# An S5 and attention network in fp32: scan result left in its PSUM bank, GpSimd's product one unit later, and reordered jobs in five stages

## Chip, core and metric

The kernel runs on one core of a Trainium2 chip. The metric is the device time of one execution in microseconds (us); of several runs the median is taken. Engines: PE is TensorE, DVE is VectorE, ACT is ScalarE, POOL is GpSimd, SP issues most DMAs.

## What is computed

Two networks one after the other, on 256 tokens (T) of 1024 features (D), all in fp32. Only the S5 mixer is shown in full; the rest is named.

```python
x = first_block(x, c, ...)    # ada-modulated: conv + retention mixer, FFN (f1.0, f2.0), S5 mixer + GLU, FFN (f1.1, f2.1)
return second_block(x, mem_2, ...)  # gated linear attention, forgetting attention, attention into mem, gates, FFN
...
def _mixer_s5(h, lam_re, lam_im, log_step, b_re, b_im, c_re, c_im, d_skip, w_glu_a, w_glu_b):
    # x_t = a * x_(t-1) + B u_t (complex diagonal a), in both directions of time; y_t = Re(C x_t) + d u_t
    ...
    return (z @ w_glu_a) * jax.nn.sigmoid(z @ w_glu_b)      # z = gelu(y)
```

## The kernel before

The program has one hand-written instruction stream per engine, with semaphores between them. On PE every job (a group of matmuls into one PSUM bank) has its place in a list (`job_order`), and bank number = turn modulo the number of banks; `begin` waits until the bank's former reader is done, and `job_wait` on another engine waits for a job's end. Weights come by DMA on SP's queue into a ring of three slots of 2 MB ("panels"). A matmul of exact fp32 value is made of three fast ones: ACT copies the high part (`split_high`, L874), DVE subtracts it for the low part (`split_low`, L1346), and `project_split` runs high x high, high x low, low x high. Every such unit thus needs ACT, then DVE, then PE.

Stages in order of time, with the span's us of the profiled execution: modulation vectors (`ada`, DVE `ada_acc` L1290/L1293), the conv and retention mixer (to about 173), its output projection `wo0` (173 to 210), the norm `ms1` (219), FFN `f1.0` and `f2.0` (230 to 470), `ms2`, the S5 mixer (482 to 573), GLU (573 to 622), `ms3`, `mk`, the second FFN (653 to 850), the projections and the attentions (850 to 1014), gates, output and last FFN.

**S5 tables.** POOL computes for each of 8 slabs k the powers of a, the x part and the c part (L711, L714, L719); PE turns them into weights (`wt{k}`, transposes) and lags (`kl{k}`, the products that make the within-block convolution), in `s5_weights(k)`, of which the jobs stand between those of `wo0`, `f1.0` and `f2.0` (`S5_AFTER`, `SIDE_S5`). They need POOL's part of that slab (`tab_step`).

**S5 loop.** `uu` puts the input h into blocks. Then come 16 units n, two for each slab k:

- PE `drive(n)`: 32 matmuls of 64x64 into bank `v{n}`.
- DVE (loop at L1531): two products of the bank with a rotation table (L1542, L1543) into `pbuf`.
- POOL (loop at L768): the add of the two (L774) into `wbuf`.
- DVE: the scan (L1553) from `wbuf` with the decay rows that ACT writes (L998) into `gbuf`; and one product of it with the table (L1557).
- POOL: the other product (L781) of `gbuf`.
- PE `outputs(n)`: 64 matmuls of 64x63 over both products, accumulated in bank 6 or 7 with the within-block part. For odd n ACT then takes GELU (L1020), and `natural(k)` (jobs `z{k}`) puts tokens in order again, for the GLU.

PE's order in the loop is `outputs(n)`, `drive(n+3)`, and for even n from 2 on `natural(n/2-1)`. POOL's and DVE's order in it is

```python
for n in range(17):      # POOL, L768
    if n < 16: ...       # wait s5p 2n+2; wbuf = pbuf[0] + pbuf[1]     (add of unit n)
    if n >= 1: ...       # m = n-1; wait s5g m+1; product of unit m
for n in range(17):      # DVE, L1531
    if n < 16: ...       # two products of unit n
    if n >= 1: ...       # m = n-1; scan and product of unit m
    if n >= 5 and n % 2: z_low((n - 5) // 2)
```

`KEEP_BUSY` names jobs before which PE multiplies into a bank nobody reads while it waits.

Of the kernel before, what the change touches and what calls it, by code (L numbers as in the profile page):

```python
# [20 lines left out]
P = 128  # L21
T = 256
# [21 lines left out]
KEEP_BUSY = {"f1.0.0": 4, "uu0": 6, "ga0": 4, "ms3": 6}  # L44
# [16 lines left out]
ADA_AFTER = {3: 10, 6: 11, 8: 12, 11: 13, 13: 14, 15: 15}  # L61
# [3 lines left out]
S5_AFTER = {4: 2, 10: 3, 15: 4}  # L65
SIDE_ADA = {0: 16, 1: 17, 3: 18, 4: 19, 5: 20, 6: 21}
SIDE_S5 = {1: 5, 3: 6, 5: 7}


def job_order():  # L70
# [4 lines left out]
            "wo0.0", "ada7", "wo0.1", "wt0.0", "kl0", "wt0.1", "ada8", "wo0.2", "ada9", "wo0.3", "wt1.0", "kl1", "wt1.1", "ms1"]  # L75
    for j in range(16):
        jobs.append(f"f1.0.{j}")
        if j in ADA_AFTER:
            jobs.append(f"ada{ADA_AFTER[j]}")
        if j in S5_AFTER:  # L80
            k = S5_AFTER[j]
            jobs += [f"wt{k}.0", f"kl{k}", f"wt{k}.1"]
    for b in range(8):
        if b in SIDE_ADA:
            jobs.append(f"ada{SIDE_ADA[b]}")
        if b in SIDE_S5:
            k = SIDE_S5[b]
            jobs += [f"wt{k}.0", f"kl{k}", f"wt{k}.1"]
    jobs += [f"f2.0.{p}" for p in range(4)] + ["ms2"]
    jobs += [f"uu{q}" for q in range(4)] + [f"v{n}" for n in range(3)] + [f"dd{q}" for q in range(4)]  # L90
    for n in range(16):
        if n + 3 < 16:
            jobs.append(f"v{n + 3}")
        if n >= 2 and n % 2 == 0:
            jobs.append(f"z{n // 2 - 1}")
        if n == 11:
            jobs.append("mms")
# [3 lines left out]
    for j in range(2, 16):  # L101
        jobs.append(f"f1.1.{j}")
        if j in (5, 9):
# [3 lines left out]
             "nr0", "nr1", "fk1", "cs0", "cs1", "at0", "at1", "go0", "gor0", "nr2", "nr3", "go1", "gor1",  # L107
             "fv0", "fv1", "mq0", "mq1"]
    bg = 0
    for u in range(10):  # L110
# [4 lines left out]
        if u in (0, 1):  # L115
            jobs.append(f"nr{4 + u}")
# [6 lines left out]
    for p in range(1, 6):  # L123
# [9 lines left out]
ROOTS = ["ms0", "rr0", "rr1", "var", "ms1", "ms2", "mms", "ms3", "mkr0", "mkr1", "ms4", "ms5", "nr0", "nr1", "gor0",  # L133
         "nr2", "nr3", "gor1", "nr4", "nr5", "ms6"]
BANKS = 6
LATE_WEIGHTS = tuple(f"{name}" for k in (5, 6, 7) for name in (f"wt{k}.0", f"kl{k}", f"wt{k}.1"))
ROTATING = [name for name in JOBS if not name.startswith("ada") and name not in LATE_WEIGHTS]
# [3 lines left out]
def build(nc, a, out):  # L141

    ctx = ExitStack()
    with ctx:
# [192 lines left out]
        ffn_panels(0)  # L337
        for i in range(2):
            cols_panel(f"ga{i}", a["w_glu_a"], 512 * i, 512, f"ga{2 * i + 1}")
            cols_panel(f"gb{i}", a["w_glu_b"], 512 * i, 512, f"gb{2 * i + 1}")  # L340
            if i == 0:
                panels.append(("mem", a["mem"].rearrange("(k p) t -> p k t", p=P), KT, T, ("memn", None)))
# [71 lines left out]
        high_bufs = [split["ada_slot0"][:, 0:2048], split["ada_slot0"][:, 2048:4096], split["prep"][:, 0:2048]]  # L414
# [63 lines left out]
        freed = {f"ms{n}": ("rstd", n + 1) for n in range(7)}  # L478
        for j in range(2):
# [5 lines left out]
                          f"go{j}": ("gon", 2 * j + 2), f"gor{j}": ("gors", j + 1), f"fv{j}": ("fvc", j + 1)})  # L485
# [21 lines left out]
        def c_steps(k):  # L507
# [5 lines left out]
                      "kot": ("koc", 1), "cs0": ("gst", 5), "cs1": ("gst", 3)})  # L513
        freed.update({f"nr{i}": ("nrs", i + 1) for i in range(6)})
# [38 lines left out]

        def ada_in(k):
# [25 lines left out]
        def _(sp):  # L580
# [3 lines left out]
            for k in range(EARLY_ADA):  # L584
                sp.dma_start(ada_slot(k), ada_source(k)).then_inc(ada_in(k)[0], 16)  # L585
# [27 lines left out]
            for i, (name, src, k, n, _) in enumerate(panels):  # L613
# [26 lines left out]
                if name == "mem":  # L640
# [12 lines left out]
        def _(pool):  # L653
# [72 lines left out]
            for k in range(8):  # L726
# [18 lines left out]
                if k:  # L745
                    pool.wait_ge(s("wout_out"), 16 * k)
                pool.wait_ge(s("tab_step"), done)
# [20 lines left out]
            for n in range(17):  # L768
# [22 lines left out]
        def _(act):  # L791
# [44 lines left out]
            def split_high(u):  # L836
# [28 lines left out]
                elif u in (GATES, GATES + 1):  # L865
# [21 lines left out]
            ada_load(act, 6)  # L887
            for j in range(2):
                job_wait(act, f"ag{j}")
# [1604 lines left out]
```

## Time and profile before

| | |
|---|---|
| median of 3 runs | 1332.55 us (1329.34 to 1334.72) |
| profiled execution | 1337.0 us, span 1335.2 us |
| mean granted PE clock | 0.956 of full |
| busy PE / DVE / ACT / POOL | 1233.7 / 856.9 / 530.6 / 410.0 us |
| HBM | 192 GB/s over the span |

All rows below are of that one profiled execution, in us from the start of its span. A row gives the start, the busy time, engine, line, operation with output<-inputs by tile, and in brackets the idle time before it and what ended that. PEclk is the granted share of TensorE's full clock. Matmuls overlap, so the step from one to the next is its cost, not its own duration.

### The profile page before, as it was taken

Reading aid. Unit: us, or ns where it says so; the run is one execution under the profiler, and the core shown is the slowest. Engines: PE = TensorE matmul, PEld = TensorE weight load, DVE = VectorE, ACT = ScalarE, POOL = GpSimd, SP = SyncE. Lnnn points to the kernel's source line nnn. Section 1 sums busy time; section 2 is a strip of 40 time slices with the busy share of each in tenths; the row PEclk is TensorE's granted clock in tenths of the full one; section 3 lists DMA queues with packets and bytes.
Section 4 is the critical chain, followed back from the end, with each engine's and each line's share of the span. In section 5 each row is a group of like instructions: output and inputs, shape, how many; then the busy total and the mean of one; then the engine's idle time right before and its main releaser. Section 6 shows DMA issues by size and latency. Waiting matters only on the chain.

```text
span 1335.2 us, 24456 instructions
## 1 busy us (share of the span) xinstructions
PE 1233.7 (92%) x10696; PEld 1143.0 (86%) x10696; DVE 856.9 (64%) x946; ACT 530.6 (40%) x663; POOL 410.0 (31%) x573
## 2 busy tenths in 40 slices
PE   4898897999998878898999999998998999999998
PEld 4785685999998848787899999698787999999998
DVE  6699963886567558845597543556856467556553
ACT  2130232444233244343455432448267644544241
POOL 7999638398788218700000000000000012000000
PEclk7899898999998889999999999999798999999999
DMA  9962667588977645256265554345141445455551
GB/s 349 389 256 94 236 219 262 187 306 304 338 286 273 225 138 172 75 171 229 68 249 190 189 179 175 122 156 190 43 147 64 151 166 189 161 174 177 182 192 64
DMA packets 120251, 258.20 MB, mean 193 GB/s; under 512 B 5056, under 2 KB 19024, under 8 KB 120016
## 3 DMA queue, kind: packets, MB, share of 16 engines
q1 hardware_dynamic: 91184, 196.18, 41.8%
q10 hardware_dynamic: 25504, 46.81, 9.6%
q0 software_dynamic: 3456, 13.63, 2.7%
q8 instruction: 85, 1.39, 0.4%
q14 instruction: 22, 0.18, 0.0%
HBM read 241.93 MB, written 14.68 MB: 192 GB/s over the span
## 4 chain that ended last, share of the span: by engine, by line
PE 68%; DVE 11%; POOL 8%; DMA 5%; issue 3%; ACT 3%; SPq 1%; DVEq 0%; POOLq 0%; ACTq 0%
PE bank L1864 68%; DVE big L1403 4%; POOL tabw L714 2%; POOL tabw L711 2%; POOL big L781 2%; DMA ring<-in_w_in 1%; DMA ada_slot<-in_ada_w 1%; DVE ada_acc L1293 1%; POOL prep L719 1%; DMA ring<-in_w_fc 1%; DVE rstd L1303 1%; POOL big L774 1%; SPq L585 1%; DVE ring_split L1346 1%; ACT ada_slot_split L874 1%
## 5 line engine op out<-in xcount | busy, mean ns | idle before, releaser
L1864 PE MATMUL bank<-squares_split,ring_split 128*128 128x256 f32 x1056 | 300.7, 285 | 0.0
L1864 PEld LDWEIGHTS bank<-squares_split,ring_split 128*128 128x128 f32 x1056 | 204.5, 194 | 0.0
L787 POOL TENSOR_TENSOR y_cat<-y_cat,tmp 128x512 f32<-128x512 f32 x8 | 11.1, 1388 | 536.9 <-DVE tmp L1782 536.9
L1293 DVE SCALAR_TENSOR_TENSOR ada_acc<-ada_slot,cact,ada_acc 128x512 f32<-128x512 f32 x152 | 126.9, 835 | 5.1
L1864 PE MATMUL bank<-ada_slot_split,ring_split 128*128 128x256 f32 x432 | 122.2, 283 | 0.0
L1346 DVE TENSOR_TENSOR ring_split<-ring,ada_slot_split 128x2048 fp32r<-128x2048 f32 (+1 forms) x32 | 72.1, 2257 | 56.9 <-ACT ada_slot_split L874 56.9
L1864 PE MATMUL bank<-big_split,ring_split 128*128 128x256 f32 x352 | 100.1, 284 | 0.0
L1303 DVE RECIPROCAL rstd<-bank 128x512 f32<-128x512 f32 (+1 forms) x21 | 56.0, 2668 | 51.1 <-ACT bank L805 51.0
L1864 PE MATMUL bank<-big_split,ada_slot_split 128*128 128x256 f32 x296 | 85.5, 289 | 0.0
L1864 PEld LDWEIGHTS bank<-ada_slot_split,ring_split 128*128 128x128 f32 x432 | 82.9, 192 | 0.0
L1346 DVE TENSOR_TENSOR ring_split<-ring,tabw_split 128x2048 fp32r<-128x2048 f32 x22 | 50.4, 2291 | 49.6 <-ACT tabw_split L874 49.6
L1864 PE MATMUL bank<-h_in_split,ada_slot_split 128*128 128x256 f32 x272 | 78.2, 287 | 3.6 <-DVE ring_split L1346 2.2
L874 ACT ACTIVATE ada_slot_split<-ring 128x2048 fp32r<-128x2048 f32 (+1 forms) x32 | 60.3, 1885 | 49.1 <-PE bank L1864 27.8
L1864 PE MATMUL bank<-h_in,ring 128*128 128x256 f32 x320 | 74.0, 394 | 2.6 <-ACT h_in L829 2.6
L1346 DVE TENSOR_TENSOR ring_split<-ring,y_cat_split 128x2048 fp32r<-128x2048 f32 x21 | 50.3, 2396 | 38.5 <-ACT y_cat_split L874 38.5
L1864 PE MATMUL bank<-big_split,tabw_split 128*128 128x256 f32 (+1 forms) x264 | 74.7, 283 | 0.0
L1864 PEld LDWEIGHTS bank<-h_in,ring 128*128 128x128 f32 x320 | 63.3, 199 | 12.0 <-issue 2.7
L1346 DVE TENSOR_TENSOR ring_split<-ring,tmp_split 128x2048 fp32r<-128x2048 f32 x20 | 47.5, 2375 | 33.0 <-ACT tmp_split L874 33.0
L1864 PE MATMUL bank<-squares_split,tmp_split 128*128 128x256 f32 x208 | 62.6, 301 | 6.1 <-DVE h_in_split L1338 5.6
L1864 PEld LDWEIGHTS bank<-big_split,ring_split 128*128 128x128 f32 x352 | 68.0, 193 | 0.0
L874 ACT ACTIVATE tabw_split<-ring 128x2048 fp32r<-128x2048 f32 x22 | 42.0, 1909 | 45.8 <-PE bank L1864 29.1
L1864 PE MATMUL bank<-squares_split,y_cat_split 128*128 128x256 f32 x208 | 59.5, 286 | 0.0
(420 smaller groups left out, 3879.9 us busy)
## 6 DMA issues: line engine op xcount, KB each, us to landing
ring<-in_w_fc SPq DMA_DIRECT2D x32, 2048.0 KB, 8.7
ada_slot<-in_ada_w ACTq DMA_DIRECT2D x20, 2048.0 KB, 10.5
ring<-in_w_in SPq DMA_DIRECT2D x19, 2048.0 KB, 8.2
ring<-in_w_ffn_gate SPq DMA_DIRECT2D x5, 2048.0 KB, 7.8
ring<-in_w_ffn_up SPq DMA_DIRECT2D x5, 2048.0 KB, 7.9
ring<-in_w_ffn_down SPq DMA_DIRECT2D x5, 2048.0 KB, 7.8
ring<-in_w_out SPq DMA_DIRECT2D x4, 2048.0 KB, 7.7
ring<-in_w_branch SPq DMA_DIRECT2D x3, 2048.0 KB, 7.8
```

What stands on the lines that cost most here:

```text
L585: sp.dma_start(ada_slot(k), ada_source(k)).then_inc(ada_in(k)[0], 16)
L711: step(pool.tensor_tensor(part.rearrange("p (d m c) -> p d m c", d=2, m=8), before, real[:, n_].rearrange("p (d q) r -> p d (q r)", d=2).u ...
L714: step(pool.tensor_tensor(both[:, 128 * d:128 * d + 128].rearrange("p (q r c) -> p q r c", q=4, r=2), one_way(view, steps, e - 1, d)[:, :, ...
L719: step(pool.tensor_tensor(by_step(view, n, steps, e), x_parts[:, 0:256].rearrange("p (d m c) -> p d m c", d=2, m=8), x_parts[:, 256:512].r ...
L774: pool.tensor_tensor(wbuf[n % 2], pb[:, 0], pb[:, 1], ALU.add).then_inc(s("s5w"), 1)
L781: pool.tensor_tensor(rotated(m)[:, 1], gbuf[m % 2][:, :, ::-1, :], tab[:, :, 2:0:-1, :], ALU.mult).then_inc(s("s5r"), 1)
L874: act.activation(high, whole, ACT.Copy).then_inc(s("w_high"), 1)
L1293: stt(acc, w[:, i, :], cact[:, i:i + 1], acc, ALU.mult, ALU.add)\
L1303: return dve.reciprocal(rs[:, 0:width], ps(job)[:, 0:width]).then_inc(s(sem), 1)
L1346: tt(low, whole, high.bitcast(F32), ALU.subtract).then_inc(s("w_low"), 1)
L1403: stt(conv[:, i, :], src, w, conv[:, i, :], ALU.mult, ALU.add).then_inc(s("conv"), 1)
L1864: return pe.matmul(*args, skip_group_check=True, **kw)
```

## The change

It has one part in the S5 loop and several in other stages.

1. S5 loop. DVE's scan writes its result into bank `v{m}` (free by then) instead of `gbuf`, and its product reads it there. ACT copies the bank to `gbuf` (`scanned`), POOL's product reads that copy, and POOL's loop takes it with m=n-2 instead of n-1. The `z` jobs use the other half of banks 6 and 7; the low parts `z_low` come two units later. PE's order in the loop is the same.
2. Before the loop. `mms` (mean square of the memory input) moves from inside the loop to ahead of `uu`; `uu` is done in two halves of the features; the memory panel is loaded earlier.
3. Start. The DMAs of the first four ada panels come in two halves; DVE's `s5_scalars` moves ahead of `ada_acc(4)`.
4. Around `wo0`. `wt` and `kl` are separate jobs, both of slab 0 ahead of `wo0.0`; `wo0.0` and `wo0.1` are interleaved (`project_pair`), as are `f1.0.0` and `f1.0.1`; `ms1` is ahead of slab 1; in `f1.0` and `f2.0` `kl{k}` stands some units behind `wt{k}`. POOL issues the DMA of the `bc` table after the x part.
5. `ms3`. ACT squares before it splits the next weights. `KEEP_BUSY` is smaller, and gone for `ga0`.
6. Projections. `fv` goes ahead of `gla_out(0)`; six roots of norms are kept in SBUF instead of a bank; DVE's order of splits and head norms is changed.

The diff, cut to its core:

```diff
-KEEP_BUSY = {"f1.0.0": 4, "uu0": 6, "ga0": 4, "ms3": 6}
+KEEP_BUSY = {"f1.0.0": 2, "uu0": 4, "ms3": 2}
...
+WT_AFTER = {2: 2, 6: 3, 10: 4, 14: 5}
+KL_AFTER = {4: 2, 8: 3, 12: 4}
...
-            "wo0.0", "ada7", "wo0.1", "wt0.0", "kl0", "wt0.1", "ada8", "wo0.2", "ada9", "wo0.3", "wt1.0", "kl1", "wt1.1", "ms1"]
+            "wt0.0", "wt0.1", "kl0", "wo0.0", "wo0.1", "ada7", "ada8", "wo0.2", "ada9", "wo0.3", "ms1", "wt1.0", "wt1.1", "kl1"]
...
         # POOL
-            for n in range(17):
+            for n in range(18):
                 if n < 16:
                     pool.wait_ge(s("s5p"), 2 * n + 2)
...
-                if n >= 1:
-                    m = n - 1
+                if n >= 2:
+                    m = n - 2
                     tab = tabs[m // 2 % 3][:, 4 * (m % 2):4 * (m % 2) + 4]
-                    pool.wait_ge(s("s5g"), m + 1)
+                    pool.wait_ge(s("s5c"), m + 1)
...
         # ACT
+            def scanned(n):
+
+                act.wait_ge(s("s5q"), n + 1)
+                if n >= 2:
+                    act.wait_ge(s("s5r"), n - 1)
+                act.activation(gbuf[n % 2].rearrange("p q c t -> p (q c t)"), ps(f"v{n}")[:, :], ACT.Copy).then_inc(s("s5c"), 1)
...
+            squares(3, False)
             split_high(SECOND)
+            root("ms3")
...
         # DVE
                     dve.wait_ge(s("s5w"), m + 1)
-                    if m >= 2:
-                        dve.wait_ge(s("s5r"), m - 1)
                     dve.wait_ge(s("decay"), 4 * m + 4)
-                    flat = (view.rearrange("p q c t -> p (q c t)") for view in (gbuf[m % 2], wbuf[m % 2]))
-                    result, source = flat
+                    source = wbuf[m % 2].rearrange("p q c t -> p (q c t)")
+                    result = ps(f"v{m}")[:, :]
                     dve.tensor_tensor_scan(result, decays[m % 3], source, 0.0, ALU.mult, ALU.add).then_inc(s("s5g"), 1)
...
-                    tt(rotated(m)[:, 0], gbuf[m % 2], tab[:, :, 0:1, :].broadcast_to([P, 4, 2, 64]), ALU.mult).then_inc(s("s5q"), 1)
-                if n >= 5 and n % 2:
-                    z_low((n - 5) // 2)
+                    scan = result.rearrange("p (q c t) -> p q c t", q=4, c=2)
+                    tt(rotated(m)[:, 0], scan, tab[:, :, 0:1, :].broadcast_to([P, 4, 2, 64]), ALU.mult).then_inc(s("s5q"), 1)
+                if n >= 6 and n % 2 == 0:
+                    z_low((n - 6) // 2)
...
         # PE
-            for i in range(2):
-                w = panel(f"wo{i}")
-                for j in range(2):
-                    project(f"wo0.{2 * i + j}", w, 2 * j, yt3, cat_ready, order=(4, 5, 6, 7, 0, 1, 2, 3))
+            s5_weights(0)
+            s5_lags(0)
+            w = panel("wo0")
+            project_pair(("wo0.0", "wo0.1"), w, yt3, cat_ready, (4, 5, 6, 7, 0, 1, 2, 3))
+            ada(7)
+            ada(8)
+            w = panel("wo1")
+            project("wo0.2", w, 0, yt3, no_wait)
+            ada(9)
+            project("wo0.3", w, 2, yt3, no_wait)
+            mean_squares(1)
+            s5_weights(1)
+            s5_lags(1)
```

**Order on POOL in the S5 loop, before** (units 2 to 5; `big` holds `pbuf`, `wbuf`, `gbuf` and the products; the second row is the first unit's product):

```order
L774 TENSOR_TENSOR big<-big 128x512 [waits s_s5p] x2
L781 TENSOR_TENSOR big<-big,tabw 128x512 [waits s_s5g]
L774 TENSOR_TENSOR big<-big 128x512 [waits s_s5g,s_s5p]
L781 TENSOR_TENSOR big<-big,tabw 128x8x64 [waits s_s5g]
L774 TENSOR_TENSOR big<-big 128x512 [waits s_s5g,s_s5p]
```

and now:

```order
L794 TENSOR_TENSOR big<-big 128x512 [waits s_s5p] x2
L794 TENSOR_TENSOR big<-big 128x512 [waits s_s5g,s_s5p]
L801 TENSOR_TENSOR big<-big,tabw 128x512 [waits s_s5c]
L794 TENSOR_TENSOR big<-big 128x512 [waits s_s5g,s_s5p]
L801 TENSOR_TENSOR big<-big,tabw 128x8x64 [waits s_s5c]
```

The first unit's product (the first row with `tabw`) had two adds ahead of it and now has three; so it goes for every unit.

**Order on PE in the S5 loop, now** (64x63 are outputs, 64x64 over `squares,ada_slot` a drive, over `squares,prep` the within-block part of an even unit, 32x64 `natural`; the 48 ahead are the drives of units 0 to 2; line L1864 of before is L1932):

```order
L1932 MATMUL bank<-squares,ada_slot 64x64 x48
L1932 MATMUL bank<-prep,s_select 128x512 x16
L1932 MATMUL bank<-squares,prep 64x64 x8
L1932 MATMUL bank<-big,ada_slot 64x63 x32
L1932 MATMUL bank<-squares,ada_slot 64x64 x16
L1932 MATMUL bank<-big,ada_slot 64x63 x32
L1932 MATMUL bank<-squares,ada_slot 64x64 x16
```

Before has the same rows in the same order: after unit 0's outputs the drive of unit 3, after unit 1's that of unit 4.

**Order on PE around `wo0`, before** (`y_cat,ring` is `wo0`, `ident,tabw` is `wt`, `prep` with 32x64 is `kl`, `one,ada_acc` is `ada`, `squares,inv` is `ms1`):

```order
L1864 MATMUL bank<-y_cat,ring 128x256 x16
L1864 MATMUL bank<-one,ada_acc 128x1 x4
L1864 MATMUL bank<-y_cat,ring 128x256 x16
L1864 MATMUL bank<-ident,tabw 64x64 x16
L1864 MATMUL bank<-prep 32x64 x16
L1864 MATMUL bank<-ident,tabw 64x64 x16
L1864 MATMUL bank<-one,ada_acc 128x1 x4
L1864 MATMUL bank<-y_cat,ring 128x256 x16
```

and now:

```order
L1932 MATMUL bank<-ident,tabw 64x64 x32
L1932 MATMUL bank<-prep 32x64 x16
L1932 MATMUL bank<-y_cat,ring 128x256 x32
L1932 MATMUL bank<-one,ada_acc 128x1 x8
L1932 MATMUL bank<-y_cat,ring 128x256 x16
L1932 MATMUL bank<-one,ada_acc 128x1 x4
L1932 MATMUL bank<-y_cat,ring 128x256 x16
L1932 MATMUL bank<-squares,inv 128x256 x8
```

Slab 0's `wt` and `kl` moved from behind `wo0.1` to ahead of `wo0.0`, and `ada8` from behind them to right behind the pair.

## Rows read from the trace of the kernel before

**Rows 1.** The page: busy time by engine, chain that ended last.

```profile
PE 1233.7 (92%) x10696; PEld 1143.0 (86%) x10696; DVE 856.9 (64%) x946; ACT 530.6 (40%) x663; POOL 410.0 (31%) x573
...
PE 68%; DVE 11%; POOL 8%; DMA 5%; issue 3%; ACT 3%; SPq 1%; DVEq 0%; POOLq 0%; ACTq 0%
```

**Rows 2.** Busy time by stage: stretch, length, busy by engine, PEclk, DMA.

```profile
200.00:243.00 43.00, 32.51 (x230) 27.13 (x229) 22.29 (x28) 12.29 (x21) 37.92 (x60) 0.84 0.58 206
400.00:470.00 70.00, 61.99 (x631) 61.10 (x630) 45.49 (x47) 19.13 (x19) 38.94 (x42) 0.90 0.69 253
500.00:574.00 74.00, 62.94 (x1836) 58.63 (x1833) 61.76 (x64) 31.67 (x79) 53.55 (x29) 0.95 0.37 115
...
626.00:654.00 28.00, 21.36 (x90) 18.13 (x89) 14.95 (x21) 14.81 (x21) 0.00 (x0) 0.88 0.23 86
930.00:1014.00 84.00, 73.59 (x392) 58.20 (x393) 62.18 (x59) 38.34 (x50) 0.00 (x0) 0.86 0.26 92
...
512.00:552.00 40.00, 33.97 (x1111) 32.09 (x1109) 37.90 (x42) 19.76 (x58) 33.80 (x18) 1.00 0.51 161
```

**Rows 3.** Timeline of PE, S5 loop: start, duration, instruction.

```profile
518.10 2.09 PE L1864 MATMUL bank<-big,ada_slot 64*64 64x63 f32 x64 [1.34 <-POOL big L781]
519.99 1.14 PE L1864 MATMUL bank<-squares,ada_slot 64*64 64x64 f32 x32
...
522.39 2.21 PE L1864 MATMUL bank<-big,ada_slot 64*64 64x63 f32 x63 [0.68 <-POOL big L781]
...
526.48 0.74 PE L1864 MATMUL bank<-big,ada_slot 64*64 64x63 f32 x18 [0.42 <-POOL big L781]
```

**Rows 4.** Timeline of DVE, the same pass.

```profile
521.17 0.69 DVE L1542 TENSOR_TENSOR big<-bank,tabw 128x512 f32<-128x512 f32 x1
...
522.37 1.22 DVE L1553 TENSOR_TENSOR_SCAN big<-ada_acc,big 128x512 f32<-128x512 f32 x1
523.62 1.58 DVE L1557 TENSOR_TENSOR big<-big,tabw 128x512 f32<-128x512 f32 x1
```

**Rows 5.** Timeline of POOL, the same pass; and L774 over the loop.

```profile
522.53 2.12 POOL L774 TENSOR_TENSOR big<-big 128x512 f32<-128x512 f32 x1 [0.29 <-DVE big L1543]
524.61 1.72 POOL L781 TENSOR_TENSOR big<-big,tabw 128x512 f32<-128x512 f32 x1
...
L774 POOL TENSOR_TENSOR big<-big x16: 1259/2115/2122, 493.1 to 559.9; 128x512 f32<-128x512 f32 x16
```

**Rows 6.** Timeline of PE: outputs(0), outputs(13), first GLU job.

```profile
499.88 0.33 PE L1864 MATMUL bank<-big,ada_slot 64*64 64x63 f32 x5
...
559.02 2.08 PE L1864 MATMUL bank<-big,ada_slot 64*64 64x63 f32 x64
...
573.52 0.57 PE L1864 MATMUL bank<-h_in_split,ada_slot_split 128*128 128x256 f32 x1
```

**Rows 7.** Timeline of PE: an outputs and a drive after a wait.

```profile
508.20 3.15 PE L1864 MATMUL bank<-big,ada_slot 64*64 64x63 f32 x64 [2.09 <-POOL big L781]
511.08 1.68 PE L1864 MATMUL bank<-squares,ada_slot 64*64 64x64 f32 x32
512.69 0.65 PE L1864 MATMUL bank<-tmp,s_select 128*32 128x64 f32 x32
```

**Rows 8.** Timeline of PE: `kl` jobs that wait for POOL.

```profile
408.88 1.08 PE L1864 MATMUL bank<-prep 128*32 128x64 f32 x32 [4.05 <-POOL prep L719]
...
442.47 1.08 PE L1864 MATMUL bank<-prep,memory_kv 128*32 128x64 f32 x32 [3.96 <-POOL prep L719]
```

**Rows 9.** Timeline of PE: `uu`.

```profile
482.19 6.77 PE L1864 MATMUL bank<-h_in,s_select 32*128 32x512 f32 x32 [4.42 <-ACT h_in L829]
```

**Rows 10.** Timelines of ACT and PE around `ms3`.

```profile
628.75 1.91 ACT L874 ACTIVATE tabw_split<-ring 128x2048 fp32r<-128x2048 f32 x1 [5.59 <-DMA ring<-in_w_fc]
...
633.03 6.44 PE L1864 MATMUL bank<-squares,inv 128*128 128x256 f32 x16 [6.63 <-ACT squares L816]
```

**Rows 11.** Timeline of PE, projections: a wait for DVE.

```profile
933.81 1.22 PE L1864 MATMUL bank<-tmp,big 128*128 128x128 f32 x4 [4.67 <-DVE rstd L1303]
```

More of the change, by code:

```diff
@@ L79, in job_order @@
             jobs.append(f"ada{ADA_AFTER[j]}")
-        if j in S5_AFTER:
-            k = S5_AFTER[j]
-            jobs += [f"wt{k}.0", f"kl{k}", f"wt{k}.1"]
+        if j in WT_AFTER:
+            jobs += [f"wt{WT_AFTER[j]}.{d}" for d in range(2)]
+        if j in KL_AFTER:
+            jobs.append(f"kl{KL_AFTER[j]}")
     for b in range(8):
@@ L85, in job_order @@
             jobs.append(f"ada{SIDE_ADA[b]}")
[L86 to L89, printed above, removed]
+        if b in SIDE_WT:
+            jobs += [f"wt{SIDE_WT[b]}.{d}" for d in range(2)]
+        if b in SIDE_KL:
+            jobs.append(f"kl{SIDE_KL[b]}")
+    jobs += [f"f2.0.{p}" for p in range(4)] + ["ms2", "mms"]
     jobs += [f"uu{q}" for q in range(4)] + [f"v{n}" for n in range(3)] + [f"dd{q}" for q in range(4)]
@@ L131 @@
 INDEX = {name: i for i, name in enumerate(JOBS)}
-ROOTS = ["ms0", "rr0", "rr1", "var", "ms1", "ms2", "mms", "ms3", "mkr0", "mkr1", "ms4", "ms5", "nr0", "nr1", "gor0",
-         "nr2", "nr3", "gor1", "nr4", "nr5", "ms6"]
+ROOTS = ["ms0", "rr0", "rr1", "var", "ms1", "ms2", "mms", "ms3", "mkr0", "mkr1", "ms4", "ms5", "nr0", "nr1",
+         "nr2", "nr3", "gor0", "gor1", "nr4", "nr5", "ms6"]
 BANKS = 6
-LATE_WEIGHTS = tuple(f"{name}" for k in (5, 6, 7) for name in (f"wt{k}.0", f"kl{k}", f"wt{k}.1"))
-ROTATING = [name for name in JOBS if not name.startswith("ada") and name not in LATE_WEIGHTS]
+LATE_WEIGHTS = ("kl5", "wt6.0", "wt6.1", "kl6", "wt7.0", "wt7.1", "kl7")
+S5_JOBS = tuple([f"v{n}" for n in range(16)] + [f"dd{q}" for q in range(4)] + [f"z{k}" for k in range(8)])
+ROTATING = [name for name in JOBS if not name.startswith("ada") and name not in LATE_WEIGHTS + S5_JOBS]
 TURN = {name: i for i, name in enumerate(ROTATING)}
@@ L475, in build @@
         mk_sq = prep[:, 2048:3072]
-        freed = {f"ms{n}": ("rstd", n + 1) for n in range(7)}
+        freed = {f"ms{n}": ("hn", 8 * n + 8) if n < 2 else ("rstd", n + 1) for n in range(7)}
         for j in range(2):
@@ L950, in _ @@
             split_high(1)
-            squares(1)
+            squares(1, False)
+            split_high(2)
+            root("ms1")
+            shift(1)
+            s5_weights_out(1)
+            s5_lags_out(1)
             ada_load(act, 11)
-            s5_weights_out(1)
-            shift(1)
-            split_high(2)
             def relus(l, after):
@@ L1003, in _ @@
                 negate(k)
-            for n in range(3):
+            decay_row(0)
+            shift(2)
+            root("mms")
+            for n in (1, 2):
                 decay_row(n)
-            shift(2)
             for q in range(2):
@@ L1034, in _ @@
+            high_part(7)
             split_high(GLU + 2)
-            root("mms")
             ada_load(act, 22)
@@ L1522, in _ @@
             norm(2)
+            dve.wait_ge(s("hn"), 24)
+            rms("mms", sem="mrs")
             for q in range(2, 4):
@@ L2201, in _ @@
                     natural(n // 2 - 1)
-                if n == 11:
-                    begin("mms")
-                    for k in range(KT):
-                        pe.wait_ge(s("msq"), k // 2 + 1)
-                        last = mm(ps("mms")[:, 0:T], inv1024, mem_sq[:, T * k:T * k + T], start=(k == 0), stop=(k == KT - 1))
-                    end(last)
             natural(7)
@@ L2326, in _ @@
             head_mean(3)
+            gla_mean(0)
             gla_out(1)
[L2328 to L2330 removed]
+            project_split("mq0", PROJ + 12, *h2, no_wait)
+            gla_mean(1)
+            project_split("mq1", PROJ + 13, *h2, no_wait)
             def gate(j):
```

374 lines of the change are left out of this document (224 added, 150 removed).

## Prediction

> **What bounds the kernel now.** I read the page first, then the busy time by stage, then the timelines of the stages in which PE is not full. PE is busy for 1233.7 us (92% of the span) and carries most of the chain that ended last [rows 1]. So an edit pays only where PE waits, or where it runs at the lower of its two clocks (2.4 and 1.2 GHz, granted 1.00 and 0.5). The stage table [rows 2] shows five such places. PE idles 10.5 us in 200:243, 8.0 in 400:470, 11.1 in 500:574, 6.6 in 626:654 and 10.4 in 930:1014. A mean clock c over w us means 2(1-c)w us at half clock. That costs at most half as much again of itself: 6.9, 7.0, 3.7, 3.4 and 11.8 us there.
>
> **The S5 loop, the part that decides.** A unit of the loop is PE `drive(n)`, DVE's two products, POOL's add, DVE's scan and product, POOL's product, PE `outputs(n)`. In the timeline of before [rows 3 to 5], one pass reads: outputs begins at 518.10; its 64 matmuls take 1.89 to the next start; the drive, from 519.99, takes 1.07. DVE's first product starts 0.11 after it, at 521.17. POOL's add starts at 522.53, the product behind it at 524.61, and the next outputs that needs this product starts at 526.48. That is 8.38 us from outputs to outputs. But the trace has another outputs in between, at 522.39. The pass is two units long, so a unit costs 4.3 us, and over 13 units with all their hitches it is (559.02-499.88)/13 = 4.55 us [rows 6].
>
> Why two units? In before POOL's product of unit n stands behind the add of unit n+1, whose drive PE issued after outputs(n-2). In the change the product stands one unit further back, behind the add of n+2 (the order of POOL above), and PE's order is the same: the drive of n+2 comes right after outputs(n-1). So outputs(n) needs product(n), which is queued behind add(n+2), which needs drive(n+2), which comes after outputs(n-1). **The same pass of 8.38 us now joins one outputs to the next, not to the next but one.** POOL is one queue and cannot overtake. ScalarE's copy, the bank and the scan are all finished a unit before: the copy lies beside POOL's add and costs nothing on this chain, at any price up to the some 5 us that it has; if it took longer, POOL's product would wait for it. DVE's last product reads a bank and no longer the SBUF tile that POOL reads. Now it takes 1.58 us [rows 4], against 0.69 for the products that read a bank. That saves DVE up to 0.9 us a unit. But DVE would then stand idle for over half of a unit, so it is worth nothing.
>
> The price of a unit lies between 8.38 us at full clock and 9.91 at half: with PE at half clock outputs takes 2.88 and the drive 1.61 (508.20, 511.08 and the row after it, 512.69, in [rows 7]), and the 5.42 us of DVE and POOL stay. PE would be busy 3.6 of 8.4 us and idle some 5 in a row. In the trace the waits of 4.05 and 3.96 us, and even the one of 2.09, are each followed by matmuls at half speed [rows 7, 8]. So I take two units of three at half clock: 9.4 us. Thirteen passes (outputs(1) to outputs(13); the last two have no add ahead of them) make 122.2 us against 59.1: +63. The Trainium skill (TensorE: Matmul & The Clock Gate, HAM oscillation) says that waits inside a loop can drop the array back to its low clock each time round. By that rule all units run at half clock and the sum is 7 us higher. The half-speed rows after waits agree with it, but no row shows a loop with 5 us holes.
>
> Ahead of the loop, the `uu` transposes in halves and `mms` in the wait before them take most of 4.42 us of idle [rows 9]. POOL's product one unit later costs outputs(0) about 2 of them: -2 net. Behind outputs(13), product(14) has no add ahead of it, and the 2.3 us that PE waited there go: 12.5 instead of 14.5 us to the first GLU job (573.52): -2. **Loop: +59 us.** Bounds: +46 (all at full clock) and +66.
>
> **The other edits**, all on waits of PE:
> - Start and `wo0`. The earlier first half of the ada panels lets DVE begin earlier than 54.92. But `kl0` stands ahead of `wo0.0` now (order of PE above) and needs POOL's table of k=0, and `ada(8)` moves ahead of `wo0.2`. The interleaved pair and the early `ms1` save what is left. Ceiling 10.5 + 6.9 = 17; I take 5, since POOL is busy 37.9 of 43 us there and stays the bound. Ends: 0 and 17.
> - `kl` apart from `wt` in the f1 and f2 stages. PE waits 4.05 and 3.96 us for POOL [rows 8]; with a unit of PE work or more between the two jobs these go, with the half clock behind them. Ceiling 8.0 + 7.0 = 15; I take 13. Ends: 5 and 15.
> - `ms3`. ScalarE waits for the DMA of `w_fc` at 628.75, splits twice, and squares only after both; PE starts at 633.03 after 6.63 us [rows 10]. In the change the squares come first. The residual is out at about 625. Ceiling 6.6 + 3.4 = 10; I take 9, and 5 as the low end (the splits are then 2 us later for f1.1.0, which has the mk jobs as cover).
> - Projections. DVE sits between PE's jobs: PE waits 4.67 us for `rstd` [rows 11]. `fv` ahead of `gla_out`, roots kept in SBUF and DVE's new order take some. Ceiling 22; I take 9.5: DVE is busy 62 of 84 us and its reciprocals are as long as before. Ends: 3 and 15.
>
> Edits that cost nothing: the DMA of `bc` later on POOL's queue (it has a stage of POOL work as cover; without it PE's `wt` would wait up to some us), fewer keep-busy matmuls (they fill waits; with shorter waits they would be in the way).
>
> **Sum:** +59 - 5 - 13 - 9 - 9.5 = +22.5. The profiled execution took 1337.0 us for a span of 1335.2; the runs shown have the median 1332.55. The differences hold for both: 1357.7 for the span, and 1332.55 + 22.5 = **1355 us** as the time.
>
> **Rivals.**
> 1. *The pass doubles, at full clock.* 13 x 8.38 = 108.9: 13 less, 1342. For it: 512:552 had full clock although POOL held PE up each unit, for 0.7 us. Against: the holes are seven times as long. 0.15.
> 2. *POOL's add gets free.* It takes 2.12 us, but only 1.26 at its shortest, and it starts just behind DVE's scan (522.37, 1.22 us): it waits for it [rows 4 to 6]. If a scan that writes to a bank held POOL no more, the pass is 8.38 - 1.05 = 7.33, at full clock 95.3: 1328. The Trainium skill (SBUF — State Buffer, Who interferes with whom) says that a DVE instruction with two SBUF inputs blocks a GpSimd instruction that reads SBUF. By that rule it makes no difference where the scan writes, since its decay row and its source both stay in SBUF; rival 2 falls by it, and the 1.58 us of the last product become 0.69. The overlaps in the rows agree. 0.08.
> 3. **Faster than before:** *the pass does not double.* The place is the POOL row of product n against add n+2; if PE's drives ran a unit ahead of what I read, PE's own work would decide (33.97 us in 40 at 4.3 us a unit: 3.65). 13 x 3.65 = 47.5 instead of 122.2: 1280. It decides if drive(n+2) is done before outputs(n-1) starts; the order rows say it is not. 0.05.
> 4. *The other edits reach their ceilings* (17+15+10+22 = 64 instead of 36.5): 1328. Against it: POOL and DVE stay busy in these stages. 0.08.
> 5. *They give half, and the loop is all at half clock:* +18 +7: 1380. 0.12.
>
> My forecast has 0.52, with 1345 to 1368 as its own range. The range to state leaves out rival 3, the far parts of 2, 4 and 5: 1336 to 1374. A measurement of this kernel tells 0.5% (6.7 us) from no change, so slower means above 1339.2. Slower: 0.52 + 0.12 + 0.11 of rival 1 = 0.75. Same: 0.04 of rival 1 and half of rivals 2 and 4: 0.13. Faster: rival 3 and the rest, 0.12.
>
> **What would show it.** In the new timeline outputs should start 8.4 to 9.9 us apart, with PE idle 4 to 5 us before each and POOL's product as its releaser, the granted clock of the loop near 0.7 and the loop about 120 us long; POOL's add still 2.1 us, DVE's last product 0.7. PE's waits for `prep` and for the squares should be all but gone. Starts under 5 us apart would make the forecast wrong at its root; starts at 8.4 with full clock would make it 13 us too high.

## The result, and the profile after

The changed kernel takes **1373.31 us** (median of 4 runs, 1370.5 to 1375.58) against 1332.88 for the kernel before in the same comparison: ratio 1.0305, 95% interval 1.0279 to 1.0331. It is slower, by 40 us. The forecast was 1355, with a range of 1336 to 1374. The two profiled executions have spans of 1335.2 and 1370.2 us; everything below that speaks of stages is made against these, a difference of 35.0. (It is less than 40 because the execution of the kernel before that was profiled, 1337.0 us, was 4 us above that kernel's median, and the profiled one of the changed kernel, 1372.01, 1.3 below its own.)

The page of the changed kernel answers to [rows 1]:

```profile
span 1370.2 us, 24505 instructions
...
PE 1236.4 (90%) x10704; PEld 1158.0 (85%) x10704; DVE 840.1 (61%) x946; ACT 536.5 (39%) x679; POOL 401.1 (29%) x573
...
PE 64%; POOL 10%; issue 7%; DVE 4%; DMA 3%; ACT 1%; SPq 1%; DVEq 0%; ACTq 0%; POOLq 0%
```

DVE is busy for less (its last product reads a bank), POOL too, and PE as long as ever. What grew is time in which PE waits. Who it waits for is in the list of PE's waits over the S5 loop alone (us in total, times, longest):

```profile
PE bank L1932 <- POOL big L801: 36.5, 9, 4.9
PE bank L1932 <- DVE y_cat_split L1594: 18.3, 5, 3.7
```

and the busy time of the loop, 491 to 633 us, with a granted clock of 0.69 (before: 0.95, [rows 2]); PE is busy there for 87 us, against 63, with nearly as many matmuls, which is the lower clock:

```profile
491.00:633.00 142.00, 87.37 (x1820) 84.14 (x1821) 51.23 (x66) 35.06 (x86) 46.77 (x28) 0.69 0.18 58
```

The milestones of both traces split the 35.0 us. `outputs(0)` starts at 491.13 instead of 499.88; the first GLU job at 631.57 instead of 573.52; `ms3` at 679.12 instead of 633.03; `ms4` at 884.26 instead of 840.90.

| stretch | before | after | change | forecast |
|---|---|---|---|---|
| start to outputs(0) | 499.88 | 491.13 | -8.75 | -20 |
| outputs(0) to first GLU job | 73.64 | 140.44 | +66.8 | +61 |
| GLU job to ms4 (ms3 in it) | 267.38 | 252.69 | -14.7 | -9 |
| ms4 to the end | 494.3 | 485.9 | -8.4 | -9.5 |

One pass of the new loop, first on PE, then DVE, ACT and POOL (an even and an odd unit; compare [rows 3 to 5]):

```profile
550.37 3.68 PE L1932 MATMUL bank<-big,ada_slot 64*64 64x63 f32 x64
553.81 1.46 PE L1932 MATMUL bank<-squares,ada_slot 64*64 64x64 f32 x32
555.20 0.65 PE L1932 MATMUL bank<-tmp,s_select 128*32 128x64 f32 x32
555.31 0.69 DVE L1607 TENSOR_TENSOR big<-bank,tabw 128x512 f32<-128x512 f32 x1 [6.30 <-PE bank L1932]
555.91 0.68 DVE L1608 TENSOR_TENSOR big<-bank,tabw 128x512 f32<-128x512 f32 x1
556.51 1.22 DVE L1616 TENSOR_TENSOR_SCAN bank<-early,big 128x512 f32<-128x512 f32 x1
556.67 2.11 POOL L794 TENSOR_TENSOR big<-big 128x512 f32<-128x512 f32 x1 [6.45 <-DVE big L1608]
557.77 0.69 DVE L1621 TENSOR_TENSOR big<-bank,tabw 128x512 f32<-128x512 f32 x1
558.49 0.60 ACT L1051 ACTIVATE big<-bank 128x512 f32<-128x512 f32 x1 [7.24 <-DVE big L1621]
558.75 1.26 POOL L801 TENSOR_TENSOR big<-big,tabw 128x512 f32<-128x512 f32 x1
560.15 1.12 PE L1932 MATMUL bank<-big,ada_slot 64*64 64x63 f32 x16 [4.30 <-POOL big L801]
```

Outputs to outputs is 9.78 us here, with every unit in it; before, 8.38 us held two. DVE stands for 6.30 us and POOL for 6.45 until the drive of the unit two ahead is done. The copy (558.49 to 559.09) serves a later unit: POOL's product of this pass has its data from the pass before, and starts in the instant that its own queue lets it.

The second row of the list of waits needs a word. In the even units from unit 4 on, the idle time of PE is put down to DVE's `z_low` (L1594), which PE needs before the within-block part of `outputs`:

```profile
589.02 1.26 POOL L801 TENSOR_TENSOR big<-big,memory_kv 128x512 f32<-128x512 f32 x1
589.21 1.12 PE L1932 MATMUL bank<-squares,prep 64*64 64x64 f32 x16 [3.67 <-DVE y_cat_split L1594]
590.43 3.68 PE L1932 MATMUL bank<-big,ada_slot 64*64 64x63 f32 x64
```

But `outputs` itself starts at 590.43, 0.15 us after POOL's product ends (590.28), as it does in an odd unit (560.01 and 560.15). So POOL's product sets the start in even units too, and `z_low` is a second tie of almost the same length beside it. The change made this tie: DVE does the `z_low` that unit n's outputs needs in its iteration n+2, and did it in iteration n+1 before. That is one unit later, and not two, as the description of the change has it.

### The profile page after: what moved, and what is told of

Its sections match the earlier page's. It is cut to its first block, busy times and chain, and to the rows that moved or that the text cites. A ratio compares the mean times of both kernels' runs of the same rounds, so it can differ in the third digit from the quotient of the medians.

```text
span 1370.2 us, 24505 instructions
## 1 busy us (share of the span) xinstructions
PE 1236.4 (90%) x10704; PEld 1158.0 (85%) x10704; DVE 840.1 (61%) x946; ACT 536.5 (39%) x679; POOL 401.1 (29%) x573
## 4 chain that ended last, share of the span: by engine, by line
PE 64%; POOL 10%; issue 7%; DVE 4%; DMA 3%; ACT 1%; SPq 1%; DVEq 0%; ACTq 0%; POOLq 0%
PE bank L1932 63%; POOL tabw L733 2%; POOL tabw L730 2%; POOL big L801 1%; DVE rstd L1365 1%; POOL big L794 1%; POOL prep L738 1%; DMA ada_slot<-in_ada_w 1%; POOL tabw L738 1%; DMA ring<-in_mem 1%; DVE ada_acc L1355 1%; DMA ring<-in_w_ffn_down 1%; DVE ring_split L1408 1%; POOL tabw L769 0%; DVE h_in L1384 0%
## 5 line engine op out<-in xcount | busy, mean ns | idle before, releaser
L1932 PE MATMUL bank<-squares_split,ring_split 128*128 128x256 f32 x1056 | 298.9, 283 | 0.0
L1932 PEld LDWEIGHTS bank<-squares_split,ring_split 128*128 128x128 f32 x1056 | 202.9, 192 | 0.0
L1932 PE MATMUL bank<-ada_slot_split,ring_split 128*128 128x256 f32 x432 | 122.2, 283 | 0.0
L1932 PE MATMUL bank<-big_split,ring_split 128*128 128x256 f32 x352 | 100.1, 284 | 0.0
L1932 PE MATMUL bank<-big,ada_slot 64*64 64x63 f32 x1024 | 55.2, 299 | 37.0 <-POOL big L801 36.5
L1932 PEld LDWEIGHTS bank<-big,ada_slot 64*64 64x64 f32 x1024 | 52.9, 210 | 39.1 <-issue 39.0
L1932 PE MATMUL bank<-big_split,ada_slot_split 128*128 128x256 f32 x296 | 84.9, 287 | 0.0
L1932 PEld LDWEIGHTS bank<-ada_slot_split,ring_split 128*128 128x128 f32 x432 | 82.9, 192 | 0.0
L794 POOL TENSOR_TENSOR big<-big 128x512 f32<-128x512 f32 x16 | 32.0, 2004 | 163.4 <-DVE big L1608 163.4
L1932 PE MATMUL bank<-h_in,ring 128*128 128x256 f32 x320 | 73.9, 394 | 1.8 <-ACT h_in L849 1.8
L1932 PE MATMUL bank<-big_split,tabw_split 128*128 128x256 f32 (+1 forms) x264 | 74.7, 283 | 0.0
L1932 PE MATMUL bank<-h_in_split,ada_slot_split 128*128 128x256 f32 x256 | 72.6, 284 | 1.2 <-issue 1.2
L1932 PEld LDWEIGHTS bank<-h_in,ring 128*128 128x128 f32 x320 | 63.2, 198 | 11.1 <-issue 1.9
L1932 PEld LDWEIGHTS bank<-big_split,ring_split 128*128 128x128 f32 x352 | 68.1, 194 | 0.0
L1932 PE MATMUL bank<-squares_split,tmp_split 128*128 128x256 f32 x208 | 59.8, 287 | 2.1 <-DVE h_in_split L1400 2.1
## 6 DMA issues: line engine op xcount, KB each, us to landing
ada_slot<-in_ada_w ACTq DMA_DIRECT2D x20, 2048.0 KB, 12.9
```

Source lines behind the costliest of these rows:

```text
L794: pool.tensor_tensor(wbuf[n % 2], pb[:, 0], pb[:, 1], ALU.add).then_inc(s("s5w"), 1)
L1932: return pe.matmul(*args, skip_group_check=True, **kw)
```

## Experiments

Theory: POOL's product n stands behind the add of n+2 in one queue, this add needs the drive that PE issues after outputs(n-1), and so each outputs waits for a full round of PE, DVE and POOL. PE's half clock then makes the round longer. Rival: the bank and ScalarE's copy, a further engine in the chain, cost the time.

**e1: only POOL's place undone.**

```diff
-            for n in range(18):
+            for n in range(17):
...
-                if n >= 2:
-                    m = n - 2
+                if n >= 1:
+                    m = n - 1
```

> The changed kernel with one edit undone: POOL takes the product of unit n-1 after the add of unit n, as before; scan result in the bank, ScalarE's copy and all other edits stay. Theory (POOL's place in its queue ties outputs(n) to the drive that follows outputs(n-1)): odd units come free of it. Even units stay tied by the wait on the low part z_low, which DVE does in the iteration of unit n+2: so two units take about 9.2 us instead of 19.2, the S5 loop from the first outputs to the first GLU job (140.4 us with the change) falls to about 75, and the time to some 1308. Rival (the bank and the copy cost the time, since POOL now waits for ScalarE after DVE): the loop stays over 110 us and the time over 1345.

Measured: 1327.17 us (ratio to before 0.9941, 0.992 to 0.9961). The loop took 92.7 us (486.65 to 579.34), granted clock 0.82. So 48 of the loop's 140.4 us went with this one edit (46 us of the time), and the rival falls: bank and copy are all still there. But the loop is 18 us longer than expected. The waits of PE in it say why (the waits on POOL that headed the list are now 2.1 us):

```profile
PE bank L1932 <- DVE y_cat_split L1594: 23.1, 6, 4.2
PE bank L1932 <- ACT prep L1068: 2.9, 1, 2.9
```

The second tie binds once the first is gone: an even outputs waits for `z_low`, which DVE does only after the products of unit n+2. With a hole of 3.4 to 4.2 us in each pair of units, the clock fell again and again: of the six even outputs from unit 4 on, five took 3.2 to 3.5 us instead of 1.9.

**e4: the second tie cut too.**

```diff
-                if n >= 6 and n % 2 == 0:
-                    z_low((n - 6) // 2)
+                if n >= 5 and n % 2:
+                    z_low((n - 5) // 2)
...
+                if 4 <= n < 16 and n % 2 == 0:
+                    high_part((n - 4) // 2)
                 if n + 3 < 16:
                     decay_row(n + 3)
```

> As e1, and the low parts z_low at odd n as before the change, with ScalarE's high parts ahead of its decay rows in an iteration so that DVE need not wait for them. Theory with the second tie: even units come free too, a pair takes about 8.1 to 8.4 us, 3 to 8 us in all less than e1. If z_low was no tie (PE's waits on it only took the place of the wait for POOL): the same as e1 within 2 us.

Measured: 1304.16 us (0.9774, 0.9744 to 0.9804), 23 us less than e1; loop 72.2 us. The direction is the theory's and so is the time it ends at (1300 to 1305 were expected). The step from e1 is three times what I had expected, because e1 was 19 us slower than I had forecast: I had priced it at full clock, and it ran at 0.82.

**e2: POOL's order as changed, but PE one drive further ahead.**

```diff
...
+            pe.wait_ge(s("ddc"), 4)
+            drive(3)
             for n in range(16):
                 outputs(n)
-                if n + 3 < 16:
-                    drive(n + 3)
+                if n + 4 < 16:
+                    drive(n + 4)
```

> The changed kernel with PE's drives one unit further ahead (drive 3 right behind the dd jobs, then outputs(n), drive(n+4)); POOL's order, copy and bank stay as in the change. Theory (the cycle goes through the drive that follows outputs(n-1)): add(n+2) now has its drive from behind outputs(n-2), both ties (POOL's queue and z_low) are cut at once, a pass again covers two units, and with DVE's and POOL's part of it 4.95 instead of 5.42 us a pair takes about 8.0 us at full clock: the loop falls from 140.4 to about 70 us, the time to about 1303. Rival (POOL's later product or the copy is slow by itself): 1345 or more.

Measured: 1297.54 us (0.9728, 0.9702 to 0.9753); loop 64.7 us, 9 us less than before the change (2.4 of them are dummy matmuls ahead of `ga0` that the changed kernel leaves out). It touches nothing of POOL, DVE or ACT and takes away the whole loss, through the other end of the same tie. PE's timeline has two units in 7.91 us again:

```profile
515.99 2.08 PE L1932 MATMUL bank<-big,ada_slot 64*64 64x63 f32 x64 [0.55 <-POOL big L801]
517.87 1.13 PE L1932 MATMUL bank<-squares,ada_slot 64*64 64x64 f32 x32
...
519.54 2.08 PE L1932 MATMUL bank<-big,ada_slot 64*64 64x63 f32 x64
...
523.90 1.29 PE L1932 MATMUL bank<-big,ada_slot 64*64 64x63 f32 x37 [0.55 <-POOL big L801]
```

**e3: the kernel before, with POOL's product one unit later and nothing else** (`range(18)`, `m = n - 2`; the scan stays in SBUF, no copy).

> The kernel before with one edit of the change alone: POOL's product one unit later (m=n-2), scan result still in SBUF, no copy, all else as before. Theory: this edit by itself costs what the loop lost, 13 units from 4.55 to about 10 us at half clock, +65 to +70 us: about 1400. Its pass keeps the 5.4 us of DVE and POOL, so it should be the slowest of all. Rival (the bank and the copy carry the loss): under 1350.

Measured: 1412.12 us (1.058, 1.054 to 1.062); loop 146.1 us, +72.5 over before. The edit alone makes the loss of the loop, without bank or copy, and with `z_low` where it was before the change. The time is 78 us over before's 1334, more than the 65 to 70 forecast. Its pass, on PE:

```profile
572.53 3.68 PE L1864 MATMUL bank<-big,ada_slot 64*64 64x63 f32 x64 [4.75 <-POOL big L781]
575.97 1.48 PE L1864 MATMUL bank<-squares,ada_slot 64*64 64x64 f32 x32
577.28 0.64 PE L1864 MATMUL bank<-squares,prep 64*64 64x64 f32 x16
582.78 2.50 PE L1864 MATMUL bank<-big,ada_slot 64*64 64x63 f32 x42 [4.86 <-POOL big L781]
```

That is 10.25 us, 5.50 of it DVE and POOL, against 4.95 in the change.

**e5 and e10: hold PE's clock up, leave the pass.** Dummy matmuls ahead of outputs(1) to outputs(12), 20 in e5 and 5 in e10:

```diff
+            def fill(n):
+
+                v = n + 3
...
+                for _ in range(20):
+                    mm(ps(f"v{v}")[:, 0:3 * P], inv1024, inv[:, :], start=True, stop=True)
```

> The changed kernel with 20 dummy matmuls of 128x384 on PE ahead of outputs(1) to outputs(12), into the bank of the next drive, which nobody reads before it is overwritten. The pass is untouched; only PE's clock is. Theory (the loop lost a part to the half clock): with the clock granted in full a unit takes 1.9 + 1.1 + 4.95 = 7.9 us instead of 10.0, the loop falls by about 26 us to 114 and the time to about 1347. Rival (the granted clock is a symptom: a unit is set by DVE and POOL alone): within 5 us of the change, or slower by the dummies.

Measured: 1450.95 us. A dummy is two matmul records and took 0.66 us, not a third of it as I had thought, so the fill was longer than the hole: a failed experiment, which told nothing.

> As e5, with 5 dummy matmuls instead of 20: in e5 one took 0.66 us at full clock, so 20 took 13 us, three times the hole they were to fill, and e5 said nothing of the clock. Five take 3.3 us, in holes of 4.3 to 4.9 us. Theory: a unit takes 7.9 instead of 10.0 us, loop about 114 us (140.4 with the change), time about 1347. Rival (clock a symptom): within 5 us of the change's 1373.

Measured: 1346.86 us, 26.5 less than the change; loop 114.65 us at a granted clock of 0.96:

```profile
491.00:606.00 115.00, 98.66 (x1906) 76.60 (x1910) 49.52 (x62) 34.41 (x86) 47.45 (x29) 0.96 0.23 72
...
540.72 2.08 PE L1932 MATMUL bank<-big,ada_slot 64*64 64x63 f32 x64 [0.55 <-POOL big L801]
...
548.63 2.08 PE L1932 MATMUL bank<-big,ada_slot 64*64 64x63 f32 x64 [0.88 <-POOL big L801]
```

Outputs 540.72 to 548.63 is 7.91 us. So of the 66.8 us, 26 are the half clock that the holes brought (140.44 - 114.65), and 41 the doubled round itself (114.65 - 73.64).

**e6: the scan result back in SBUF, without the copy, drives ahead as in e2.**

```diff
-                    result = ps(f"v{m}")[:, :]
+                    result = gbuf[m % 2].rearrange("p q c t -> p (q c t)")
...
-                    pool.wait_ge(s("s5c"), m + 1)
+                    pool.wait_ge(s("s5g"), m + 1)
```

> As e2 (drives one unit ahead), but the scan result in SBUF as before the change, no copy by ScalarE, POOL's product straight behind the scan. So it measures bank and copy with the tie cut. Theory: DVE's last product and POOL hold each other up again (1.58 and 1.72 us instead of 0.69 and 1.27), and the pass of two units gets 0.45 us longer: loop 64.7 to about 68, time +2 to +4 us over e2. Rival (the copy costs as much as the bank saves): the same as e2 within 1 us.

Measured: 1299.71 us (0.9751, 0.9719 to 0.9784), +2.2 to e2, with intervals that overlap. The durations do come back (groups by line of the loop, mean ns):

```profile
L801 POOL TENSOR_TENSOR big<-big,tabw 128x512 f32<-128x512 f32 x12 | 20.2, 1686 | 1.2 <-DVE big L1609 1.2
L1614 DVE TENSOR_TENSOR big<-big,tabw 128x512 f32<-128x512 f32 x11 | 16.5, 1499 | 0.4
```

and a pair of units takes 8.37 us (530.20 to 538.57) instead of 7.91, yet the whole loop takes 64.15 against 64.7. Up to outputs(8) e2 is 0.9 us ahead; behind it PE stands for 2.61 us for which the profile shows no cause ("issue"), and the next outputs begins at the lower clock:

```profile
529.37 0.34 PE L1932 MATMUL bank<-squares,ada_slot 64*64 64x64 f32 x5 [2.61 <-issue]
529.64 0.65 PE L1932 MATMUL bank<-tmp,s_select 128*32 128x64 f32 x32
530.22 3.14 PE L1932 MATMUL bank<-big,ada_slot 64*64 64x63 f32 x64
```

e6 has no such hole. Why e2 has it is open, and so these runs can't tell what bank and copy together are worth from nothing.

**e7: squares of the residual ahead of those of the memory input, at ms2.**

```diff
+            squares(2, False)
             act.wait_ge(s(f"panel{place['mem'] % RING}"), 16 * (place["mem"] // RING + 1))
...
-            squares(2)
+            root("ms2")
```

> As e2, but ScalarE squares the residual for ms2 ahead of the memory input, and that one ahead of ms2's root. In the change PE waits 4.95 us for ms2's squares, since ScalarE squared the memory input first (2.2 us of it). Theory: 2 us of that wait and some of the half clock behind it go: e2 less 2 to 4 us. If the residual on DVE and not ScalarE's order ends the wait: same as e2.

Measured: 1289.89 us, 7.6 less than e2 (5.9 of them ahead of outputs(0)). In the change ScalarE stood on the DMA of the memory panel, ahead of the squares that PE needed:

```profile
459.81 2.19 ACT L1017 ACTIVATE ring<-ring 128x512 f32<-128x512 f32 x4 [17.30 <-DMA ring<-in_mem]
461.91 2.17 ACT L836 ACTIVATE squares<-x_res 128x512 f32<-128x512 f32 x4
...
462.66 5.25 PE L1932 MATMUL bank<-squares,inv 128*128 128x256 f32 x16 [4.95 <-ACT squares L836]
```

I had read the wait as ScalarE's 2.2 us of work; it was a wait for a DMA, and all 4.95 us and the half clock went.

**e8: kl0 behind the pair of wo0, ada7 ahead of it.**

```diff
             s5_weights(0)
-            s5_lags(0)
+            ada(7)
...
-            ada(7)
+            s5_lags(0)
             ada(8)
```

> As e2, but kl0 behind the pair wo0.0/wo0.1 instead of ahead of it, and ada7 ahead of the pair instead of behind it. In the change PE waits 9.95 us there for POOL's part of slab 0, and 6.97 us for DVE, which sat idle 26 us for ada7's result. Theory: both waits go, less the wait for the inputs of wo0: e2 less 8 to 15 us, if POOL's later slabs do not then bind (PE's waits for prep would grow in the f1 stage). Rival (POOL is the bound of the stage, and what is won here is waited for at kl1 to kl3): e2 less under 3 us.

ScalarE's copy of `kl0` moves too, behind its four Silu. Measured: 1290.91 us, 6.6 less than e2, between theory and rival. The two waits of the change, shown here, went; a new one of 14.55 us came at ada9, whose panel ScalarE had asked for only behind its copy of kl0:

```profile
175.33 1.08 PE L1932 MATMUL bank<-prep 128*32 128x64 f32 x32 [9.95 <-POOL prep L738]
...
199.52 1.62 PE L1932 MATMUL bank<-one,ada_acc 128*128 128x1 f32 x7 [6.97 <-DVE ada_acc L1355]
```

```profile
202.52 1.87 PE L1932 MATMUL bank<-one,ada_acc 128*128 128x1 f32 x8 [14.55 <-DVE mod L1360]
```

**e11: ScalarE's order at ms3 as before the change** (two splits, then squares), drives ahead as in e2.

> As e2, with ScalarE's order around ms3 as before the change (two splits ahead of the squares and the root). Theory: the new order is what took the wait of 6.63 us and the half clock there: e2 plus 4 to 9 us. Rival (the panel w_fc now lands in time, since the earlier DMA of the memory panel shifted the ring, so the order alone no longer matters): e2 plus 3 us or less.

Measured: 1302.18 us, 4.6 more than e2: the low end of the theory. PE waits 3.51 us again, but no longer for the DMA of `w_fc` behind it:

```profile
604.61 1.90 ACT L894 ACTIVATE tabw_split<-ring 128x2048 fp32r<-128x2048 f32 x1
606.41 1.90 ACT L894 ACTIVATE y_cat_split<-ring 128x2048 fp32r<-128x2048 f32 x1
608.21 2.17 ACT L836 ACTIVATE squares<-x_res 128x512 f32<-128x512 f32 x4
...
608.88 5.41 PE L1931 MATMUL bank<-squares,inv 128*128 128x256 f32 x16 [3.51 <-ACT squares L836]
```

So less than half of the 14.7 us between GLU and ms4 is this order; the rest came with it from elsewhere (the wait for `w_glu` of 2.2 us and the one for `w_fc` are gone). That the earlier memory panel shifted the ring is likely, but no run took it back alone.

**e9: all that helped.** e2 with e7 and e8, and ScalarE's loads of ada panels 9 and 10 ahead of its copy of kl0:

```diff
-            s5_lags_out(0)
             ada_load(act, 9)
             ada_load(act, 10)
+            s5_lags_out(0)
```

> A version meant to be faster than both kernels: e2 with the edits of e7 and e8 together, and ScalarE's issue of the loads of ada panels 9 and 10 ahead of its copy of kl0 (in e8 DVE stood 21 us without the panel, and PE 14.55 us at ada9). Theory (the waits are in different stages and each is on PE's path): the gains of e7 and e8 add up, and the load in time gives another 3 to 8 us: 1275 to 1283. Rival (POOL's slabs bind in the f1 stage once wo0 is done earlier): 1284 or more.

Measured: **1269.87 us** (5 rounds, 1264.79 to 1272.8), ratio to before 0.9524, 0.95 to 0.9549. It beats both kernels, and the change by 103 us; PE runs from the pair to the last of wo0 and into ms1 with no wait:

```profile
168.62 14.06 PE L1933 MATMUL bank<-y_cat,ring 128*128 128x256 f32 x64
182.62 0.65 PE L1933 MATMUL bank<-prep 128*32 128x64 f32 x32
183.20 1.05 PE L1933 MATMUL bank<-one,ada_acc 128*128 128x1 f32 x8
184.11 7.15 PE L1933 MATMUL bank<-y_cat,ring 128*128 128x256 f32 x32
191.10 0.95 PE L1933 MATMUL bank<-one,ada_acc 128*128 128x1 f32 x8
191.91 7.15 PE L1933 MATMUL bank<-y_cat,ring 128*128 128x256 f32 x32
198.90 3.62 PE L1933 MATMUL bank<-squares,inv 128*128 128x256 f32 x16
```

ms1 starts at 198.90 instead of 218.57 in the change. The gain over e2 is 27.7 us, where 7.6 + 6.6 + 3 to 8 were expected, and 1269.87 lies below the 1275 to 1283 of the theory. The excess stands at the load of the ada panels: ms1 starts 14.7 us earlier than in e8 (213.56), where 3 to 8 had been expected of it.

## Why the prediction held, and where it was off

**The result: inside the range by 0.7 us.** 1373.31 is in 1336 to 1374, but outside 1345 to 1368, which was the forecast's own range. By spans the change is +35.0 where +22.5 was forecast: the start is off by 11.3 us, the loop by 5.8, the last stretch by 1.1, and the stretch with ms3 by 5.7 the other way. That this one made up for the loop is luck; the mechanism of the loop is not.

**The pass that doubles: right.** Outputs start 8.7 to 10.3 us apart, POOL's product is what each waits for, POOL's add still takes 2.11 us. e1, e2 and e3 show the cause from three sides: undo POOL's place, move PE's drive, or make POOL's edit alone. Rival 3 (the pass does not double) falls with the first row. So does rival 2 (POOL's add gets free): it takes as long beside a scan that writes into a bank as it did beside one that wrote to SBUF. (The 1.05 us of that rival comes from no row; the add's 2.12 less its shortest 1.26 is 0.86. And its chances for "same" add up to 0.12, not 0.13.) Rival 1 (full clock) falls with the granted 0.69. The prediction did not see the second tie, `z_low`. It did not need it for the time, since POOL's tie is as long; e1 shows that it alone would have cost about 20 us of the loop (92.7 against 72.2 in e4).

**"Outputs takes 2.88 and the drive 1.61 at half clock": this step was mis-sized.** At half clock outputs takes 3.44 us, start to start (550.37 to 553.81). The row that I read 2.88 from [rows 7] began at full clock, which one duration does not tell; the busy time by stretch of the kernel before does (PEclk is the third figure from the end):

```profile
508.20:508.90 0.70, 0.70 (x23) 0.70 (x25) 0.70 (x1) 0.00 (x0) 0.70 (x1) 0.98 1.07 367
508.90:512.30 3.40, 3.40 (x71) 3.40 (x68) 1.93 (x2) 0.00 (x0) 3.09 (x2) 0.50 0.24 94
```

The drive was too low as well: in a unit that is slow throughout it takes 1.88 us (515.11 to 516.99), not 1.61. Against that, DVE's and POOL's part is 4.95 and not 5.42, because POOL's product takes 1.26 us instead of 1.72; I had counted the bank's gain for DVE only. A slow unit is thus 3.43 + 1.88 + 4.95 = 10.26 us (511.68 to 521.94), and not 9.91: ten of the thirteen passes are above what I had called the upper end. A unit came to (621.07-491.13)/13 = 10.0 us, not 9.4, and the thirteen passes to +70.8, not +63. Behind outputs(13) it was -4.0 and not -2, of which 2.4 are the dummy matmuls ahead of `ga0` (571.13 to 573.52), which I had counted as worth nothing. So the loop gave +66.8 and not +61. "Two units of three at half clock" was too kind: 13 of the 14 outputs from unit 0 to 13 take 3.4 us. The Trainium skill (TensorE: Matmul & The Clock Gate, HAM oscillation) has it that waits in a loop drop the clock each time round. The trace agrees, with all but one of these outputs slow. e10 gives the price, 26 us.

**"I take 5", "I take 13", "-2" ahead of the loop: off by 11 us.** The f1 and f2 stages (from the start of `f1.0.0` until PE is free for ms2) gave 10.8 of 13. But everything ahead of `f1.0.0` gave 1.8 of 5: PE came to `var`, its last job of the mixer, 12.5 us earlier (159.00 instead of 171.52), and then at `kl0`, moved ahead of `wo0`, it waited 9.95 us for POOL. I had named this wait and the next, 6.97 us at `ada(8)`, and counted them too low. I had also said that the waits for `prep` and for squares would be all but gone, and they are 10.7 and 15.6 us, against 12.9 and 17.2 before. And I had no term for ms2: the memory squares moved ahead of `squares(2)` stand on a DMA. I wrote what the edit removes (`mms` out of the loop) and not what it puts in front of another job on ScalarE's queue. This cost 5.0 us of wait, and 7.6 us by e7; the stretch from PE's arrival at ms2 to outputs(0) came out 3.8 us longer, and not 2 shorter.

**ms3 and projections:** -14.7 for -9, of which the order of squares and splits is 4.6 (e11); -8.4 for -9.5. There a new wait of 9.99 us for `tabw` at 1014.32 took the place of the old ones; no run was made on it, nor on the edits of this stage one by one.

**What the other edits are worth** shows when the loop is mended: e2 is 36 us faster than before, 9 of them in the loop. The other 27 belong to these edits together; alone, only the order at ms3 was measured (e11).

## What to carry to other kernels

When a stage of a software pipeline moves one unit later in an in-order queue, follow what now stands ahead of it, back to the engine that closes the ring: if the producer's lead does not grow by the same unit, a wait that was shared by two units is paid by each. Give the lead first (here one more drive ahead), then the delay. And price a hole in PE's work with the half clock that follows it: here the clock was 26 of 67 us, and a few dummy matmuls, sized from their own rows, won it back.

## Not expected of the hardware

The hold-up between DVE and POOL went both ways. POOL's product took 1.72 us in before and 1.26 in the change, DVE's last product 1.58 and 0.69, with the same sizes and operations; what changed for both is that DVE's scan result lies in a bank. In before the two overlap (DVE's product runs from 523.62 to 525.20, POOL's begins at 524.61); in the change DVE's has ended at 558.46 when POOL's begins at 558.75. So I read POOL's gain as DVE's product no longer holding it up; no run separates this from ScalarE's copy, which came with it. POOL's add stayed at 2.11 behind the scan, whose two inputs are in SBUF in both. With the operand back in SBUF (e6) the means were 1.69 and 1.50 again.
